# Differential tables: moved from a stage of their own into the projection of the memory, with their gate steps moved to the differential heads

## What is computed

```python
bias = rel_bias.astype(jnp.float32)[rel_bucket(rel)].transpose(2, 0, 1)
s = jnp.where(rel >= 0, s + bias[None, :, None], -jnp.inf)
p = jax.nn.softmax(s, axis=-1)
a = p[:, :, 0] - lam * p[:, :, 1]
```

## Time and profile before

| What | us |
|---|---|
| Median of three runs | 3236.74 |
| Time of the profiled execution | 3238.5 |
| Its span | 3236.7 |
| PE busy | 3002.5 (93%) |
| Projection, from the start | 0 to 582 |
| Retention | 582 to 734.2 |
| Tables | 734.5 to 787.9 |
| Differential heads of the prompt | 788.2 to 915.5 |

### The profile page before, as it was taken

How to read it: one execution, slowest core, us unless ns; L and a number is a source line. 1 busy time by engine, 2 the same in 40 slices (tenths; PEclk the granted TensorE clock), 3 DMA queues, 4 the chain that set the end, 5 groups by cost and what they waited for, 6 DMA issues and landing times. The chain is left out here.

```text
span 3236.7 us, 52374 instructions
## 1 busy us (share of the span) xinstructions
PE 3002.5 (93%) x21012; PEld 2791.7 (86%) x21012; DVE 1836.0 (57%) x2568; ACT 1274.2 (39%) x1408; POOL 1023.1 (32%) x551
## 2 busy tenths in 40 slices
PE   7999999897879784999899999999999999999998
PEld 6999999775778663999899999999999788888886
DVE  5444444472221005554539899888875567776764
ACT  5323323342533233443334453455544333333332
POOL 0000000233435330003308898877777001111000
PEclk9999999997999896999899999999999999999999
DMA  6545445564566533666767899999999888888764
GB/s 219 166 158 174 160 157 173 176 206 141 147 217 210 185 101 102 207 212 194 163 128 189 199 249 228 251 270 263 294 287 313 294 297 305 319 306 311 271 216 169
DMA packets 449260, 698.29 MB, mean 216 GB/s; under 512 B 30973, under 2 KB 345757, under 8 KB 421566
## 3 DMA queue, kind: packets, MB, share of 16 engines
q1 hardware_dynamic: 399774, 555.91, 55.8%
q10 hardware_dynamic: 40128, 73.42, 8.1%
q0 software_dynamic: 9216, 67.11, 5.6%
HBM read 627.14 MB, written 63.70 MB: 213 GB/s over the span
## 5 line engine op out<-in xcount | busy, mean ns | idle before, releaser
L2555 POOL TENSOR_TENSOR peer_uT_low<-peer_uT,peer_uT_high 128x1024 fp32r<-128x1024 f32 x256 | 615.6, 2430 | 260.9 <-ACT peer_uT_high L2582 260.3
L1017 POOL TENSOR_TENSOR gate_low<-gate_raw,gate_high 128x512 fp32r<-128x512 f32 x192 | 251.3, 1332 | 951.9 <-ACT gate_high L973 951.5
L2455 PE MATMUL banks<-x_high,peer_uT_high 128*128 128x256 f32 x2048 | 493.3, 283 | 10.0 <-ACT peer_picks_T L2614 7.8
L2456 PE MATMUL banks<-x_low,peer_uT_high 128*128 128x256 f32 x2048 | 488.8, 280 | 0.0
L2455 PEld LDWEIGHTS banks<-x_high,peer_uT_high 128*128 128x128 f32 x2048 | 386.4, 189 | 11.3 <-ACT peer_uT_high L2582 8.3
L2456 PEld LDWEIGHTS banks<-x_low,peer_uT_high 128*128 128x128 f32 x2048 | 385.6, 188 | 0.0
L247 PE MATMUL banks<-x_high,win_high 128*128 128x288 f32 (+1 forms) x1312 | 349.1, 296 | 0.0
L248 PE MATMUL banks<-x_low,win_high 128*128 128x288 f32 (+1 forms) x1312 | 348.7, 295 | 0.0
L2582 ACT ACTIVATE peer_uT_high<-peer_uT 128x1024 fp32r<-128x1024 f32 x256 | 261.7, 1055 | 100.4 <-DVE peer_uT L2705 99.9
L217 ACT ACTIVATE win_high<-win_raw 128x2048 fp32r<-128x2048 f32 x84 | 160.8, 1914 | 334.7 <-DVEq L210 329.4
L2705 DVE STREAM_TRANSPOSE peer_uT<-peer_u 128x1024 f32<-128x1024 f32 x192 | 234.1, 1230 | 84.9 <-DMA peer_u<-in_peer_u_dram 62.0
(11 more groups left out here) (398 smaller groups left out, 6549.6 us busy)
## 6 DMA issues: line engine op xcount, KB each, us to landing
win_raw<-in_w_in_dram SPq DMA_DIRECT2D x38, 2048.0 KB, 8.1
peer_u<-in_peer_v_dram SPq DMA_DIRECT2D x64, 1024.0 KB, 5.3
peer_area<-in_peer_v_dram SPq DMA_DIRECT2D x64, 1024.0 KB
gate_raw<-in_w_in_dram SPq DMA_DIRECT2D x96, 512.0 KB, 4.3
peer_u<-in_peer_u_dram SPq DMA_DIRECT2D x192, 256.0 KB
peer_u<-in_peer_u_dram ACTq DMA_DIRECT2D x192, 256.0 KB
w_raw<-in_w_up_ret_dram SPq DMA_DIRECT2D x8, 2048.0 KB, 9.2
w_raw<-in_w_out_dram SPq DMA_DIRECT2D x8, 2048.0 KB, 8.5
```

Of the source, the lines that this page charges most:

```text
L1017: pool.tensor_tensor(self.low[:, p % 2, c, :, :], self.raw[:, p % 4, :, c * P:(c + 1) * P], self.high[:, p % 2, c, :, :], ALU.subtract).th ...
L2455: pe.matmul(out, UH[:, c, k, :], XH[:, k, 0:DENSE], start=(k == 0), stop=False)
L2456: pe.matmul(out, UH[:, c, k, :], XL[:, k, 0:DENSE], start=False, stop=False)
L2555: pool.tensor_tensor(UL[:, m % 2, part, :], UT[:, m % 2, part, :], UH[:, m % 2, part, :], ALU.subtract).then_inc(low, 1)
```

## The change

The block of tables goes. A class `DiffTables` has its parts, and they are called at places of other blocks.

- The 14 loads follow the loads of x in the projection's queue. Their scratch lies in `branch_outputs`, which is empty then.
- The eight products become one with 8 rows of result (`products`, behind quarter n = 1): no 128 equal rows are made on chip. The copy (`keep`) and the samples' product follow.
- One store of 2 MB replaces eight of 256 KB (`store_rows`): its source is the 8 rows, each read 128 times, its destination the same `bias_rows`. It is queued behind the second half of `w_mem_v` and ahead of the first store to `mem_T`.
- ACT's exponential comes in quarter n = 3, DVE's weights too.
- The skewed load of 1.5 MB is issued by SP in the last head of retention, into tiles of values that are used up; DVE waits for it at the first differential head.
- The 8 ticks go to the heads: (1, 2) becomes (2, 2).
- The first block raises 56 semaphores instead of 45, and `renew` 38 instead of 31.

```diff
-TICKS_TABLES, TICKS_DIFF, TICKS_DIFF_SAMPLE, TICKS_MEM, TICKS_MEM_SAMPLE = 8, (1, 2), (3, 3), (2, 2), (2, 2)
+TICKS_DIFF, TICKS_DIFF_SAMPLE, TICKS_MEM, TICKS_MEM_SAMPLE = (2, 2), (3, 3), (2, 2), (2, 2)
-        signals = Signals(nc, top, 45)
+        signals = Signals(nc, top, 56)
...
+                    if h == last_head:
+
+                        sp.wait_ge(scaled, after(6))
+                        diff.load_bias(sp, bias, bias_loaded)
                     sp.wait_ge(pstate_ready, after(h + 1))
...
                     sp.dma_start(x_rows[0:r, t, :], x_in[t]).then_inc(x_loaded[t], 16)
+                diff.load(sp)
                 for b in range(2):
                     w.load(sp, 1, b, [w_mem[1][:, :, b * 2 * P:(b + 1) * 2 * P]])
+                diff.store_rows(sp)
                 sp.wait_ge(projected, after(1))
                 sp.dma_start(S["mem_T"][0:4].rearrange("k p t -> p k t"), out[:]).then_inc(stored, 16)
...
                         act.activation(root[:, 2:5], ms[:, 2:5], ACT.Sqrt).then_inc(x_steps, 1)
+                        diff.exponentials(act)
...
+                    if n == 1:
+                        diff.products(pe)
...
+                    if n == 0:
+                        diff.pick(dve)
                     if n == 2:
                         dve.wait_ge(squared, after(5))
                         rstds(slice(2, 5), x_steps)
+                        diff.keep(dve)
+                    if n == 3:
+                        diff.weights(dve)
...
+    def store_rows(self, sp):
+        sp.wait_ge(self.kept, after(1))
+        sp.dma_start(self.dram, self.rows.unsqueeze(1).to_broadcast([DIFF_HEADS, P, 512])).then_inc(self.rows_stored, 16)
...
+    def products(self, pe):
+        pe.wait_ge(self.ones_row, after(1))
+        pe.wait_ge(self.loaded, after(16 * len(self.loads)))
+        pe.wait_ge(self.picked, after(2))
+        pe.matmul(self.PS[0:DIFF_HEADS, 2, :], self.rb, self.buckets, start=True, stop=True)
+        pe.matmul(self.PS[:, 3, 0:PAST + NEW], self.picks, self.buckets_new, start=True, stop=True).then_inc(self.biased, 1)
...
             @block.vector
             def _(dve):
+                dve.wait_ge(bias_loaded, after(16))
                 with dve.Fori(0, DIFF_HEADS) as h:
```

More of the change, by code:

```diff
@@ L302, in decoder_step_kernel @@
                 x_high, x_low = (tensor(during_attention, "right", f"x_{part}", [P, KT, T], F32R) for part in ("high", "low"))
-                tables = retention_tables(C, ODM)
-                input_projections(nc, G, Z, x_high, x_low, tables)
-                attention(nc, G, Z, ODM, x_high, x_low, tables)
+                tables = RetentionTables(C, ODM)
+                diff = DiffTables(nc, G, during_attention, ODM)
+                input_projections(nc, G, Z, x_high, x_low, tables, diff)
+                attention(nc, G, Z, ODM, x_high, x_low, tables, diff)
             OTH = tensor(right, "right", "o_high", [P, O_TILES, T], F32R)
@@ L436, in __init__, with retention @@
         self.pick = table("pick_token", NEW)
-def retention_tables(C, ODM):
-    return RetentionTables(C, ODM)
-def retention(nc, G, Z, tables, gates, finished):
+def retention(nc, G, Z, tables, diff, bias, bias_loaded, gates, finished):
     PS, ident, ones, A, O = (G[k] for k in ("PS", "ident", "ones", "A", "O"))
@@ L710, with input_projections @@
 Z_COUNT, MEM_COUNT = Z_TILES // 4, 2
-def input_projections(nc, G, Z, XH, XL, tables):
+def input_projections(nc, G, Z, XH, XL, tables, diff):
     A, S, C, PS, ident, ones = (G[k] for k in ("A", "S", "C", "PS", "ident", "ones"))
@@ L876, in _ @@
                     w.product(pe, n // 4, n % 4, [(PS[:, n % 2, 0:MEM_TOKENS], 0, (XH[:, :, 0:MEM_TOKENS], XL[:, :, 0:MEM_TOKENS]))])
+                    if n == 1:
+                        diff.products(pe)
                     if n == 5:
                         pe.wait_ge(x_scaled_ready, after(3))
+                        pe.wait_ge(diff.kept, after(3))
                     for k in {5: range(0, 6), 6: range(6, 12), 7: range(12, 16)}.get(n, ()):
@@ L1150, in diff_prompt @@
+def diff_prompt(nc, G, Z, OD, v_new, bias, bias_loaded, map_weights, gates):
     PS, ident, O = (G[k] for k in ("PS", "ident", "O"))
@@ L1868, in _, with attention @@
                     dve.scalar_tensor_tensor(out=heads[g], in0=heads[g], scalar=ws[:], in1=rstd2[:, g], op0=ALU.mult, op1=ALU.mult)
-def attention(nc, G, Z, ODM, x_high, x_low, tables):
+def attention(nc, G, Z, ODM, x_high, x_low, tables, diff):
     OD, OM = ODM[:, 0:DIFF_HEADS, :], ODM[:, DIFF_HEADS:, :]
@@ L1876, in attention @@
         gates = GateStream(nc, G, outer, x_high, x_low)
-        retention(nc, G, Z, tables, gates, finished)
+        bias = unused[:, 4608:4608 + DIFF_HEADS * (SEQ + P)].rearrange("p (h t) -> p h t", h=DIFF_HEADS)
+        (bias_loaded,) = Stage(nc, G, outer, "attention").sems("bias_loaded")
+        retention(nc, G, Z, tables, diff, bias, bias_loaded, gates, finished)
         with ExitStack() as ctx:
@@ L1880, in attention @@
             v_new = unused[0:NEW, 0:DIFF_HEADS * P]
-            bias = unused[:, 1024:1024 + DIFF_HEADS * (SEQ + P)].rearrange("p (h t) -> p h t", h=DIFF_HEADS)
-            bias_new, bias_own, map_weights, row_weights = diff_tables(nc, G, st, bias, gates)
-            diff_prompt(nc, G, Z, OD, v_new, bias, map_weights, gates)
+            diff_prompt(nc, G, Z, OD, v_new, bias, bias_loaded, diff.map_weights, gates)
             pages = unused[:, 1024:1024 + 8192].rearrange("p (w s g c) -> p w s g c", w=2, s=2, g=N_PAGES)
-            diff_sample(nc, G, Z, OD, v_new, bias_new, bias_own, row_weights, pages[:, 0], pages[:, 1], gates)
+            diff_sample(nc, G, Z, OD, v_new, diff.bias_new, diff.bias_own, diff.row_weights, pages[:, 0], pages[:, 1], gates)
         with ExitStack() as ctx:
```

167 lines of the change are left out of this document (67 added, 100 removed).

## The result

The changed kernel takes 3247.88 us (median of 8 runs, 3244.39 to 3252.72), the kernel before 3237.15 in its 8 runs. The ratio is 1.0033, 95% interval 1.0022 to 1.0044: slower by a third of a per cent, as forecast (3245.6). The profiled execution has 3252.72 us and a span of 3250.9, against 3236.7 before.

What follows compares the result with a forecast made beforehand. PE, busy 93% of the span, was taken as the bound. Without the projection -22.4, projection +31.3, sum +8.9: 3247.4 against the profiled execution, 3245.6 against the median; own range 3240 to 3252, extended down to 3213.

Steps and rivals of the forecast that it cites:

- What goes: Block of tables between retention and heads, 734.53 to 788.21, disappears; ACT starts the heads at 735.0 instead of 788.21: -53.2 us.
- the term of +0.4: Longer first block, 3 more semaphore increments per engine: 0 to 0.6 us, taken as +0.4.
- Heads: Differential heads: eight added ticks of 3.2 us plus waits for banks, +28.7 us; heads of 18.7 us.
- the wait for the banks of 1.49: Each head's first tick waits 1.49 us for ACT to empty the banks; head 7 was to grow +3.0.
- The store's rate: 2 MB store in the projection from 8 partitions: 6.6 GB/s per partition, 52 GB/s, 40 us.
- The stall: Projection: PE's quarter 6 waits for `mem_T` behind the store until 93.7 instead of 64.89, +28.8; with cold clock +31.3.
- the cold clock: Projection: after 27 us of idleness PE runs at half clock for some 5 us, +2.5.
- As transfers of one queue go in order: SP's queue in the projection: first `mem_T` store can't be done before the 2 MB store, landing at about 93.2.
- Rival 1: Projection's narrow read not slow enough to matter, PE never waits if the store lasts under 12.6 us: 3215.7, chance 0.22.
- Its half about the engines: Rival 1's variant: only the number of DMA engines is cut, to 8; 185 GB/s, 11.3 us, 3216.
- Rival 2: Projection's store slow, but half as slow: 105 GB/s, 20 us, sum -11.5, 3225.2 us; chance 0.06.
- Rival 3: Heads grow otherwise: 6 us smaller if ticks fill PE's waits, 4 larger if ACT or POOL paces; inside range 3240 to 3252.

Runs made afterwards that it cites:

- steps of 4: Changed kernel, but the store reads its eight rows from partitions 0, 4, ..., 28, each 128 times, instead of 0 to 7: 3215.08 us.
- the wide store: Changed kernel, but the 2 MB store reads each of 128 partitions 8 times instead of each of 8 partitions 128 times: 3216.7 us, ratio 0.9944 to the kernel before.

## Why the prediction was right, point by point

- **What goes.** Right: -54.06 measured, -53.2 predicted. The barrier did not wait noticeably for POOL's 7 more increments. The price of an increment was put slightly too low by its own rows: 2.79 us for 11 or 12 of them on an engine is up to 0.25, not 0.2. On the first block the term of +0.4 came true: SP's first issue is at 3.25 instead of 2.79.
- **Heads.** The mechanism was right in all heads, the size in all but the last. Head 0 with its cold clock (transposes 1.54 us, as forecast about twice 0.87) grew by 29.13 - 24.25 = 4.9, as predicted (3.2 + 1.7). Heads 1 to 5 grew by 18.6 for a predicted 18.5, head 6 by 4.0 for 4.0. Head 7, to the samples' first work, grew by 4.5, where 3.0 was predicted. The term that was mis-sized there is the wait for the banks of 1.49: in the last head PE has no transposes and products of a next head to do while ACT empties them, and the wait was 3.02.
- **The store's rate.** 49 GB/s for 52: right in size, but not for its reason. The step divided 210 GB/s by 32 partitions. The runs show that partitions don't count: 0, 4, ..., 28 are eight too, and move 208. For 8 and 16 neighbours the rate does double with the partitions (49 and 98), so the proportion held where it was used: the right size was luck, and it would have given the same 52 for steps of 4. The sentence on the Trainium skill's page "SBUF — State Buffer", which had it by ports (38 us), named the mechanism; the store took some 43.
- **The stall.** +33.15 for 31.7 at the start of retention. The chain is the one forecast: `mem_T` behind the store, DVE's copy behind `mem_T`, quarter 6 behind the copy. The term that was short is the store's length. It came 3.7 us later at quarter 6 (97.36 for 93.7), since 49 GB/s give 43 us, not 40, and the weights ahead of the store ended nearer to 52 than to 51.3. In return the cold clock cost less: between quarter 6 (+32.47) and retention (+33.15) only 0.7 was added, not 2.5. The two errors offset each other in part, which is luck as well.
- **"As transfers of one queue go in order."** This sentence was wrong as it stands. Weights queued behind the store were moved while it ran (176 GB/s at 76 to 80), and another queue did not free `mem_T` either (PE still stood for 20.19 us). What mostly kept a later transfer from ending is its share on the busy DMA engines; its place in the queue was worth 10.6 of 37.6 us. What followed from the sentence, `mem_T` behind the store, held.
- **Rival 1** would have held from 12.6 us down. The runs put a point on each side: at 208 GB/s (10 us) 3215.08, at 98 (21 us) 3225 to 3230. Its number, 3215.7, is what the wide store gave (3216.7). Its half about the engines was right as well: eight rows kept half of them busy, and that alone cost nothing that shows (3215.08 with half of them, 3216.7 with all).
- **Rival 2** forecast 3225.2 for a store of 20 us. 21 us gave 3224.82, 3227.14 and 3229.82.
- **Rival 3** did not come: POOL did not pace the heads, ACT's order did. POOL's wait showed only once ACT's two were gone.

## What to carry to other kernels

A store whose source lies on few partitions is priced by its bytes over the ports that these partitions reach, some 25 GB/s for each here: rows that are read again and again belong on 128 partitions, or, for eight rows, on steps of 4. Here such a transfer held back whatever needed its DMA engines behind it, from its own queue and from another, and moving it changed who waited more than for how long; so ask of each small source how long it holds the engines before asking where it stands. And when work is moved into a loop, look at the helper engine's order within the loop: three moves of ACT's small steps were worth 26 us there, more than the 20 that the change brings once its store is mended. When such a kernel is taken apart, check the parts and not only the total: two forecasts here had the time right and the heads wrong.

## What the runs showed of the hardware that was not expected

- The rate of reads from SBUF went by ports of 24.5 to 26 GB/s (table above). The Trainium skill's page "SBUF — State Buffer", section "Door 1: The DMA port swizzle", gives 27.2 for each; these runs were 4 to 10% below it. Only reads from SBUF to DRAM in packets of 2 KB were measured.
- Eight source rows kept 0.46 to 0.54 of the DMA engines' time busy at 49, 98 and 208 GB/s, and 16 rows kept 0.94 busy at 98: a busy DMA share says little about the rate.
- A store at 49 GB/s on half of the engines held back a 0.5 MB store on another queue until 86, 31 us after its issue.
